# Provisional means in the layer norms, another job order in w_in, and unused identity products on TensorE before its waits

## The reference

```python
def rms_norm(x, g):
    xf = x.astype(F32)
    y = xf * lax.rsqrt(jnp.mean(xf * xf, axis=-1, keepdims=True) + EPS)
    return (y * g.astype(F32)).astype(x.dtype)

def layer_norm(x, g, b):
    xf = x.astype(F32)
    xc = xf - jnp.mean(xf, axis=-1, keepdims=True)
    y = xc * lax.rsqrt(jnp.mean(xc * xc, axis=-1, keepdims=True) + EPS)
    return (y * g.astype(F32) + b.astype(F32)).astype(x.dtype)
```

## Time and profile before

| | us |
|---|---|
| median of 3 runs | 3657.47 (3651.36 to 3661.37) |
| the profiled execution | 3652.16 |
| its span, first to last instruction | 3650.4 |
| mean granted clock of TensorE | 0.973 |

### The profile page before, as it was taken

One profiled execution on the slowest core, in us unless ns is written; L12 is line 12 of the kernel. 1 busy time (PEld: TensorE's weight loads), 2 busy tenths in 40 slices (PEclk: granted clock), 3 DMA queues, 4 the chain that ended last, 5 costly groups with the idle time before them and its releaser, 6 DMA issues.

```text
span 3650.4 us, 46045 instructions
## 1 busy us (share of the span) xinstructions
PE 3366.3 (92%) x18273; PEld 2711.7 (74%) x18273; DVE 2010.4 (55%) x3181; ACT 1310.8 (36%) x1966; POOL 409.1 (11%) x376
## 2 busy tenths in 40 slices
PE   6987899999989888999999878999999889989998
PEld 5765678888877556787787557888888766668886
DVE  3665456635547655868633765573554465555344
ACT  4334433212224453323233553421221644444232
POOL 2002460000000040000000550000000023300000
PEclk8997999999999999999999999999999999999999
DMA  5430043433422103555511012243343121123332
GB/s 180 149 117 18 4 81 103 135 101 116 136 71 64 52 1 94 156 162 171 151 57 53 11 31 65 90 133 114 104 133 88 45 44 30 33 64 101 96 102 72
DMA packets 477237, 321.79 MB, mean 88 GB/s; under 512 B 54872, under 2 KB 450558, under 8 KB 477024
## 3 DMA queue, kind: packets, MB, share of 16 engines
q1 hardware_dynamic: 467104, 304.13, 28.5%
q0 software_dynamic: 9920, 14.71, 1.6%
HBM read 313.20 MB, written 3.57 MB: 87 GB/s over the span
## 4 chain that ended last, share of the span: by engine, by line
PE 79%; DVE 8%; ACT 6%; DMA 3%; issue 3%; POOL 0%; SPq 0%; DVEq 0%; ACTq 0%; POOLq 0%
PE PS L1059 76%; PE PS L1357 3%; DMA RAW<-in_w_gate 1%; DVE CPROD L2597 1%; ACT SPH L1647 1%; DVE TMP L2354 1%; DVE CACC L2676 1%; ACT BIG L1838 1%; DVE ATT L2425 1%; DMA RAW<-in_w_in 1%; DVE HL L2338 1%; DVE X L2292 0%; ACT TMP L1838 0%; DMA RAW<-in_w_down 0%; ACT TMP L1764 0%
## 5 line engine op out<-in xcount | busy, mean ns | idle before, releaser
L1059 PE MATMUL PS<-HH,SPH 128*128 128x512 f32 (+1 forms) x3424 | 1181.3, 358 | 72.6 <-ACT SPH L1647 18.6
L1059 PE MATMUL PS<-HL,SPH 128*128 128x512 f32 (+1 forms) x3424 | 1137.3, 355 | 5.3 <-DVE HL L2338 5.3
L1059 PEld LDWEIGHTS PS<-HH,SPH 128*128 128x128 f32 x3424 | 655.5, 191 | 190.7 <-issue 57.9
L1059 PE MATMUL PS<-HH,SPL 128*128 128x512 f32 (+1 forms) x3424 | 743.5, 357 | 0.0
L1059 PEld LDWEIGHTS PS<-HL,SPH 128*128 128x128 f32 x3424 | 646.9, 191 | 96.1 <-DVE HL L2338 8.6
L2232 DVE TENSOR_TENSOR SPL<-RAW,SPH 128x1024 fp32r<-128x1024 f32 (+3 forms) x367 | 458.1, 1248 | 423.5 <-ACT SPH L1647 423.1
L1059 PEld LDWEIGHTS PS<-HH,SPL 128*128 128x128 f32 x3424 | 583.3, 191 | 101.1 <-issue 9.6
L1647 ACT ACTIVATE SPH<-RAW 128x1024 fp32r<-128x1024 f32 (+3 forms) x367 | 394.2, 1074 | 715.9 <-PE PS L1059 463.8
L1059 PE MATMUL PS<-MH,SPH 128*128 128x512 f32 (+1 forms) x1056 | 360.9, 355 | 4.7 <-ACT SPH L1647 4.7
L1059 PE MATMUL PS<-ML,SPH 128*128 128x512 f32 (+1 forms) x1056 | 358.6, 354 | 0.0
L2529 DVE SCALAR_TENSOR_TENSOR X<-PS,MOD,X 128x512 f32<-128x512 f32 (+1 forms) x144 | 95.3, 662 | 402.3 <-PE PS L1059 400.6
(11 more groups left out here) (322 smaller groups left out, 3349.5 us busy)
## 6 DMA issues: line engine op xcount, KB each, us to landing
MS<-in_mod_turned SPq DMA_DIRECT2D x144, 512.0 KB, 3.7
...
```

The source lines that it names most:

```text
L1059: return pe.matmul(o, a, b, start=start, stop=stop)
```

## The change

Three things are edited. (1) `keep_clock(n, bank)` makes PE multiply the identity with itself n times; the product is not used. It is called in the start, in front of the waits of `rms_sums` and behind its sums, behind the sums of `layer_norm_sums`, ahead of tile 2 of some linear layers (`pause`), in head norms, ahead of the lead of layer 2, behind query sums, and in attention entries ahead of the first scores and between the first steps. (2) The layer norm's mean is taken of chunks 0 and 1 behind tile 2; chunks are centred by it, squared and added up behind the tiles; at the seam only chunk 7 is left. The rest of the mean (the shift) is summed apart: the variance is corrected by its square (a subtraction), and DVE adds it to chunks 0 and 1, POOL to 2 to 7. (3) In w_in of block 0 jobs, reads and taps stand in another order, and the Silu of the conv is made at tile 19, before V2 and V3 are read.

The core of the diff, each line twelve spaces to the left (left out: semaphores and calls that only pass names on):

```diff
-STAT_USES = ["sum K0", "sum K1", "sum K2", "sum K3", "mean G", "sum G", "sum Q0", "turn G0", "turn G1", "sum Q1", "gate 0",
-         "sum Q2", "gate 1", "sum Q3", "mean C", "turn V0", "turn V1", "sum C", "turn V2", "turn V3"]
+STAT_USES = ["sum K0", "sum K1", "sum K2", "sum K3", "mean G", "sum G", "turn G0", "sum Q0", "turn G1", "sum Q1", "gate 0",
+         "sum Q2", "gate 1", "sum Q3", "mean C", "sum C", "turn V0", "turn V1", "turn V2", "turn V3"]
...
 SQUARES = ["K0", "K1", "K2", "K3", "G", "G", "Q0", "Q1", "Q2", "Q3", "C", "C"]
 MID = {5: ["sum K0"], 6: ["sum K1"], 7: ["sum K2"], 8: ["sum K3"], 9: ["w_s"], 10: ["mean G"], 11: ["sum G"],
-   13: ["sum Q0", "turn G0"], 14: ["sum Q1"], 15: ["sum Q2"], 16: ["sum Q3"], 18: ["turn V0"]}
-END = {13: ["turn G1"], 14: ["gate 0"], 15: ["gate 1"], 17: ["mean C"], 18: ["turn V1", "sum C"], 19: ["turn V2"]}
-TAPS_AT = [{4: 7, 5: 4, 6: 4, 7: 4, 8: 4, 9: 5, 10: 5, 11: 6, 12: 5, 13: 3, 14: 3, 15: 3, 16: 4, 17: 5},
-       {4: 8, 5: 5, 6: 5, 7: 5, 8: 2, 9: 2, 10: 4, 11: 5, 12: 3, 13: 2, 14: 2, 15: 2, 16: 8, 17: 9}]
+   13: ["turn G0"], 14: ["turn G1"], 15: ["gate 0"], 16: ["gate 1"], 17: ["mean C"], 18: ["sum C"], 19: ["turn V1"]}
+END = {13: ["sum Q0"], 14: ["sum Q1"], 15: ["sum Q2"], 16: ["sum Q3"], 18: ["turn V0"], 19: ["turn V2"]}
+TAPS_AT = [{4: 7, 5: 5, 6: 5, 7: 5, 8: 5, 9: 5, 10: 5, 11: 6, 12: 5, 13: 4, 14: 4, 15: 3, 16: 3},
+       {4: 8, 5: 6, 6: 6, 7: 5, 8: 3, 9: 3, 10: 5, 11: 5, 12: 4, 13: 4, 14: 4, 15: 4, 16: 5}]
...
-def add_pair(T):
-    pool.wait_ge(S.sq_single, w.seen(S.sq_single, DC) - 3)
-    pool.tensor_tensor(HLF[:, 3, 0:T], HLF[:, 3, 0:T], HLF[:, 4, 0:T], ALU.add).then_inc(S.pool_pair, 1)
+def shift_chunks(T):
+    pool.wait_ge(S.shift_copied, w.seen(S.shift_copied))
+    for c in range(2, DC):
+        pool.tensor_tensor(X[:, c, 0:T], X[:, c, 0:T], HLF[:, 7, 0:T], ALU.add).then_inc(S.shifted, 1)
...
+        if li == 3:
+            shift_chunks(TOK)
...
+def keep_clock(n, bank):
+    for _ in range(n):
+        mm(bank[:, 0:P], IDENT, IDENT, True, True)
...
-def linear(x, hi, lo, also=None, ready=None, order=range(DC), mid=None, chunk=None, spare=False, between=None):
+def linear(x, hi, lo, also=None, ready=None, order=range(DC), mid=None, chunk=None, spare=False, between=None, pause=0):
     def body(j, t, s):
+        if j == 2:
+            keep_clock(pause, AUX)
...
+    keep_clock(10, LIN[0])
     pe.wait_ge(S.sq_added, w.seen(S.sq_added))
     token_sums(T, STAT, TMP[2], True, True).then_inc(S.token_var, 1)
     w.seen(S.inverse_ready)
-def layer_norm_sums(T):
-    rs_read()
+    keep_clock(15 if T == TOK else 11, LIN[0])
+def first_mean(T):
     pe.wait_ge(S.mean_in, w.seen(S.mean_in))
     token_sums(T, AUX, TMP[0], True, True).then_inc(S.mean_done, w.one(S.mean_done))
-    squared = w.taken.get(S.sq_single, 0)
-    w.seen(S.sq_single, DC)
-    for c in (0, 1, 2, 5):
-        pe.wait_ge(S.sq_single, squared + c + 1)
-        token_sums(T, STAT, HLF[:, c, :], c == 0, False)
-    pe.wait_ge(S.pool_pair, w.seen(S.pool_pair))
-    token_sums(T, STAT, HLF[:, 3, :], False, False)
-    pe.wait_ge(S.dve_pair, w.seen(S.dve_pair))
-    token_sums(T, STAT, HLF[:, 6, :], False, True).then_inc(S.token_var, 1)
+def layer_norm_sums(x, T):
+    rs_read()
+    shift = shift_place(x)
+    pe.wait_ge(S.tile_free, x.t0 + 7)
+    pe.wait_ge(S.mean_in, w.seen(S.mean_in))
+    token_sums(T, shift, TMP[0], True, False)
+    pe.wait_ge(S.squares_in, w.seen(S.squares_in))
+    token_sums(T, STAT, TMP[2], True, False)
+    pe.wait_ge(S.centered, w.seen(S.centered, DC))
+    token_sums(T, shift, X[:, 7, :], False, True).then_inc(S.mean_done, w.one(S.mean_done))
+    pe.wait_ge(S.sq_single, w.seen(S.sq_single, DC))
+    token_sums(T, STAT, square_place(x, 7), False, True).then_inc(S.token_squares, 1)
     w.seen(S.inverse_ready)
+    keep_clock(15 if T == TOK else 10, AUX)
...
+    keep_clock(8 if A.mla else 10 if A.diff else 3, STAT if A.mla else AUX)
...
+        if n < 3:
+            keep_clock(((13, 0, 0) if A.mla else (9, 7, 7) if A.diff else (8, 8, 0))[n], STAT if A.mla else AUX)
         if n + 1 < len(A.steps):
...
-        for part in range(2):
-            turn_rows(1 + part)
+        turn_rows(1)
+        keep_clock(20, STAT)
+        turn_rows(2)
...
+        keep_clock(7, LIN[0])
...
+        keep_clock(12, LIN[0])
...
+            if n == 4:
+                keep_clock(8, AUX)
...
-        linear(L["w_in"], HH, HL, None, S.h_ready, mid=latent_jobs)
...
         query_spread(n0 + 1)
+        keep_clock(14, AUX)
...
+    def mean_after(j):
+        if j == 2:
+            first_mean(T)
+    linear(L["w_out"], HH, HL, mean_after if blk == 1 else None, S.mix_ready, (0, 1, 6, 7, 2, 3, 4, 5), between=head_norm if blk == 0 else None, pause=12 if blk == 0 else 0)
     pe.wait_ge(S.tile_free, L["w_out"].t0 + 8)
-    (rms_sums if blk == 0 else layer_norm_sums)(T)
+    if blk == 0:
+        rms_sums(T)
+    else:
+        layer_norm_sums(L["w_out"], T)
...
         def next_layer(j):
+            if blk == 1 and half and j == 2:
+                first_mean(T)
...
-def inverse_root(T):
-    act.wait_ge(S.token_var, w.seen(S.token_var))
+def inverse_root(T, var):
     act.wait_ge(*w.last)
-    act.activation(TMP[2][:, 0:T], STAT[:, 0:T], ACT.Ln, scale=1.0 / D, bias=EPSB).then_inc(S.act_step, w.one(S.act_step))
+    act.activation(TMP[2][:, 0:T], var[:, 0:T], ACT.Ln, scale=1.0 / D, bias=EPSB).then_inc(S.act_step, w.one(S.act_step))
...
-def layer_norm_inverse(T):
-    for c in range(DC):
-        act.wait_ge(S.centered, w.seen(S.centered))
-        act.wait_ge(*w.last)
-        act.activation(HLF[:, c, 0:T], X[:, c, 0:T], ACT.Square).then_inc(S.sq_single, w.one(S.sq_single))
-    inverse_root(T)
+    act.wait_ge(S.token_var, w.seen(S.token_var))
+    inverse_root(T, STAT)
...
+def square_centered(x, T, c):
+    act.wait_ge(S.centered, w.seen(S.centered))
+    act.wait_ge(*w.last)
+    act.activation(square_place(x, c)[:, 0:T], X[:, c, 0:T], ACT.Square).then_inc(S.sq_single, w.one(S.sq_single))
+def squares_behind(x, T, also=None):
+    def evac(j, t, s):
+        if also:
+            also(j, t, s)
+        for c in {4: (0, 1), 5: (2, 3, 4), 6: (5,), 7: (6,)}.get(j, ()):
+            square_centered(x, T, c)
+    return evac
+def layer_norm_inverse(x, T):
+    shift = shift_place(x)
+    square_centered(x, T, 7)
+    act.wait_ge(S.mean_done, w.seen(S.mean_done, 2))
+    act.activation(TMP[1][:, 0:T], shift[:, 0:T], ACT.Square, scale=D ** -0.5).then_inc(S.shift_squared, 1)
+    act.activation(HLF[:, 7, 0:T], shift[:, 0:T], ACT.Copy, scale=-1.0 / D).then_inc(S.shift_copied, 1)
+    act.wait_ge(S.var_ready, w.seen(S.var_ready))
+    inverse_root(T, TMP[2])
 def make_h_normed(T, li, k):
...
-            if j == 14:
-                read_stat("turn G1", turned_g(1))
             if 5 <= j < 9:
                 inverse(f"K{j - 5}")
             if j == 11:
                 inverse("G")
-            if 13 <= j < 17:
-                inverse(f"Q{j - 13}")
-            if j == 13:
-                read_stat("turn G0", turned_g(0))
+            if 14 <= j < 18:
+                inverse(f"Q{j - 14}")
+            if j in (13, 14):
+                read_stat(f"turn G{j - 13}", turned_g(j - 13))
             if j == 18:
                 act.wait_ge(S.conv_centered, li + 1)
                 square_of("C", [big(16), big(17)])
+            if j == 19:
+                inverse("C")
                 act.wait_ge(S.norm_used, norm_at(li, "Q3") + 1)
-                read_stat("turn V0", turned_v(0))
-            if j == 19:
-                read_stat("turn V1", turned_v(1))
-                inverse("C")
+                for c in range(2):
+                    read_stat(f"turn V{c}", turned_v(c))
...
+            if j == 19:
+                act.preload_act_table_set(SILU)
+                for n in range(2):
+                    act.wait_ge(S.conv_scaled, 2 * li + n + 1)
+                    act.activation(big(16 + n)[:, 0:T], big(16 + n)[:, 0:T], ACT.Silu, bias=par(li, "cbb", n))\
+                        .then_inc(S.act_step, w.one(S.act_step))
+                act.preload_act_table_set(LOG_EXP)
         linear(L["w_in"], evac, early)
         for c in range(2):
             gated_hi(c)
         read_stat("turn V2", turned_v(2))
-        act.preload_act_table_set(SILU)
+        act.wait_ge(*w.last)
+        act.activation(HH[:, 6, 0:T], big(16)[:, 0:T], ACT.Copy).then_inc(S.mixed_hi, 1)
         read_stat("turn V3", turned_v(3))
-        for n in range(2):
-            act.wait_ge(S.conv_scaled, 2 * li + n + 1)
-            act.activation(big(16 + n)[:, 0:T], big(16 + n)[:, 0:T], ACT.Silu, bias=par(li, "cbb", n))\
-                .then_inc(S.act_step, w.one(S.act_step))
-            act.wait_ge(*w.last)
-            act.activation(HH[:, 6 + n, 0:T], big(16 + n)[:, 0:T], ACT.Copy).then_inc(S.mixed_hi, 1)
-        act.preload_act_table_set(LOG_EXP)
```

(71 more changed lines are left out.)

41 lines of the change are left out of this document (24 added, 17 removed).

## The result

The changed kernel takes 3630.4 us (median; 3628.7 to 3632.1) against 3657.5 us: ratio 0.9927, interval 0.9916 to 0.9939. That is 27 us less. It lies inside the range that was given and on the side that was forecast, but it is only half of the 53 us of the sum.

A forecast was written before the change was run, and what follows sets the result against it. TensorE (PE), busy 92% of the span, bounds the kernel; its idle time (284 us) and half clock (197 us) can be won. Terms sum to -53.1: 3652.2 becomes 3599.1, plus 5.3 for the median, 3604 us; range 3574 to 3632.

The forecast's parts named there:

- Rival B: Products don't pay: the clock falls anyway or they stand on the path as often as in gaps; 3626 us, chance 0.17.
- rival D: Slower: uncovered products delay ready work on PE and the clock gives nothing; 3690 us, chance 0.04.
- rival E: Waits in w_in only move to gates and Q sums, seams' extra work costs what seams save; 3650 us, chance 0.06.
- The terms for w_out, the RMS seams and the five single places (-14.6): Products keep the clock up: w_out of layers 0 and 1 -6.6, RMS-norm seams -1.4, five places in later layers -6.6 us.
- The start, -6.5: Twenty products fill PE's 5.8 us wait, so some 13 us of short PE chains at half clock halve: -6.5 us.
- w_in of layer 0, -17.2: New job order removes 14.5 of 14.8 us of PE waits, clock gives 4.7, new lateness costs 2.0: -17.2 us.
- late next: +2.0: In w_in of layer 0, new waits expected at turn V0's read and at the gates behind DVE's taps: +2.0 us.
- w_in of layer 1: Waits of 3.2 + 3.0 and 3.4 us of half clock go; sums Q2, Q3 wait 3.1 and 2.4: -4.1 us.
- Entries: Differential attention entries: earlier Silu delays turn V3, products cost time but raise the clock; layer 0 +0.7, layer 1 +3.4 us.
- The means, -14.8: Provisional means shorten layer-norm seams: -13.8, -3.6 and -4.4, less 7.0 for POOL's corrections beside DVE: -14.8 us.
- +0.83 on POOL or +0.56 on DVE for each meeting: In layer-norm seams, the slowdown when POOL's corrections and DVE's operations overlap, in us; 7.0 us in all.
- Rival A: POOL and DVE exclude each other fully in the seams, so the means give back 16.5 us; 3614 us, chance 0.20.

The follow-up runs named there:

- experiment 4: The changed kernel without any identity product: 3655.2 us, ratio 0.9999 to the kernel before.
- experiment 5: The kernel before with the identity products alone, same places and counts: 3633.8 us, ratio 0.9939.
- Experiment 8: The changed kernel with 25 instead of 20 products in the start and 8 more ahead of the first norm's sums: 3628.8 us.
- Experiment 10: The changed kernel with ACT's inverses of Q0 to Q3 in w_in moved ahead of the split of weights: 3622.9 us.
- experiment 7: The changed kernel with the conv's Silu and its table loads back behind the read of turn V2: 3622.1 us.
- experiments 1 and 2: The changed kernel with POOL's six seam additions cut to one token each: 3610.9 us; the changed kernel with layer norms as before: 3630.8 us.
- Experiment 6: The changed kernel with one operand of DVE's seam additions and (all seams but the last) multiplications read from PSUM: 3616.7 us.
- experiment 12: The changed kernel with DVE's seam operands in PSUM, Silu behind V2's read and Q inverses ahead of the split: 3597.0 us.

## Why the prediction was right and wrong

- **Bound and clock.** Right. PE's idle time and its clock were the two things to win, and the products in front of waits are the part that pays: 25 us by experiment 4, 21 by experiment 5. Rival B (the products don't pay) and rival D (they cost) fall, though B's time, 3626, was the nearest. For the other two parts together rival E's outcome came true, without the products they gave nothing, and for w_in its mechanism too: waits moved to the Q sums. In the seams it was another, POOL and DVE meeting. The terms for w_out, the RMS seams and the five single places (-14.6) came out at -15.2 in the pair of profiles, the entries at +3.5 for +4.1.
- **The start, -6.5.** Wrong. The step "these halve" took for granted that a filled gap keeps the clock for the whole chain behind it. It kept it for some 6 us, worth 2.0 us; then the clock fell, and the seven products in front of the lead ran at half clock and took 0.9 us back. The pair of profiles shows no gain at all (57.3 to 57.5 us), but counted from the last matmul ahead of the products all traces show 0.2 to 2.4. Experiment 8 moved the fall once more and gained nothing that the medians can tell.
- **w_in of layer 0, -17.2.** The step that failed is "late next: +2.0". The waits of the earlier trace rows went, as forecast, but 11.8 us of new ones came: 9.2 for the reads of the Q sums, which the sum had at nothing, and 2.6 for C's. I had followed the order of PE's and DVE's jobs and not that of ACT, where the read moved behind a split that waits for a DMA. Experiment 10 moves it ahead of the split: layer 0's stage then comes out as forecast, though layer 1's loses 2.5 us, and 7.5 us are left. w_in of layer 1 was near (-3.1 for -4.1), but one term of it does not follow from its rows: with a granted clock of 0.99, give some 3 us at half clock, and so 1.6 us to gain, not 3.4.
- **Entries.** The net sizes held (+0.9, +2.6 in the profiles), in part by luck: the expectation of experiment 7 took 4 us for the Silu's place from these terms, and it cost 8. That cost is avoidable.
- **The means, -14.8.** The way to Ln was right, and so was the value without meetings (21.8 against 19.9 us by experiments 1 and 2). The mis-sized term is "+0.83 on POOL or +0.56 on DVE for each meeting", 7.0 in the sum; it is about 20. It was taken from POOL's multiplications by a column (L956, one tile read), where the earlier trace rows show it; POOL's additions read two tiles, and beside them each DVE operation on two tiles grew by 1.35 us (2302 against 949 ns) and each addition of POOL by 0.6 (2.40 against 1.82). And the two additions ahead of the inverse, which I had hidden behind Ln and Exp, take 4.48 us for 1.81 and hold back the first multiplication in every seam. Rival A had this mechanism; its price of 16.5 was 3 short, and as the forecast stood its total, 3614, was 16 short for the other two misses. By the rule of the Trainium skill ("SBUF — State Buffer", Who interferes with whom) the two exclude each other fully, and the sum would have been 10 us higher. That is the better number here: 0.95 and 1.82 us one after the other make 2.77, the rounds measured take 2.4. Experiment 6 agrees with the rule's condition too: with one of DVE's operands in PSUM the same work beside the same POOL additions isn't slowed.
- **The whole.** All three misses lie on one side, 6.7 + 8.7 + 17.8 = 33 us; 3 us of unforecast gain in layer 1's feed-forward, which is luck of one execution by the spread above, and a profiled execution of before that was 5 us quick made the median's miss 26. The range held the time because it reached to rival B, though not for B's reason, and that is luck too. Of the signs that the prediction named, the mean clock came out (0.987), the start's didn't (0.88 for over 0.9), a long seam took 17.2 us for at most 12.5, and over 10 us of waits were left in w_in of layer 0, which it had called wrong. The sign for rival A, POOL's additions at over 2.9 us, was badly chosen: they took 2.4 and A's mechanism was there. With the seams, the Silu and the Q reads mended and the start as it is (experiment 12), the kernel is at 3597, 7 us below the forecast.
